# A fourth size class for experts of 65 to 96 tokens in a mixture-of-experts layer

## The reference

```python
logits = h @ w_router + b_router                 # h (320, 1024), 32 experts
top_val, top_idx = lax.top_k(logits, 4)
gates = softmax(top_val)
for each expert e, on the tokens that chose it:
    gu = xb @ w_gu[e] + b_gu[e]                  # 1024 -> 2048
    x_glu, x_lin = jnp.split(gu, 2, axis=-1)     # each clipped to 7
    act = x_glu * sigmoid(1.702 * x_glu) * (x_lin + 1.0)
    out = (act @ w_down[e] + b_down[e]) * gate   # 1024 -> 1024
    acc = acc.at[tok].add(out)
x = x + ga2 * acc
```

## Time and profile before

| what | value |
|---|---|
| time, median of 3 runs | 1476.66 us |
| profiled execution: its span, first to last instruction | 1473.6 us |
| TensorE matmuls busy | 1254.8 us, 85% |
| VectorE, ScalarE busy | 375.8 us, 217.6 us |
| bytes moved by DMA | 454.63 MB, mean 309 GB/s |
| instruction-fetch packets on queue q8 | 34, of 0.56 MB |
| chain that ended last | PE 68%, DMA 10%, SPq 7%, DVE 7%, issue 5% |

### The profile page before, as it was taken

One profiled execution on the slowest core, in us unless ns is written; L12 is line 12 of the kernel. 1 busy time (PEld: TensorE's weight loads), 2 busy tenths in 40 slices (PEclk: granted clock), 3 DMA queues, 4 the chain that ended last, 5 costly groups with the idle time before them and its releaser, 6 DMA issues.

```text
span 1473.6 us, 26636 instructions
## 1 busy us (share of the span) xinstructions
PE 1254.8 (85%) x10191; PEld 679.3 (46%) x10192; DVE 375.8 (26%) x1023; ACT 217.6 (15%) x482; POOL 29.3 (2%) x51
## 2 busy tenths in 40 slices
PE   3999999878677888788879998889999989978894
PEld 2677766653343334344434445344444443444442
DVE  1114435342111322111322123112222212321123
ACT  1323242131010101101101011010111111100100
POOL 0001110010000000000000000000000000000000
PEclk8999998887878989799989999999999999989996
DMA  9941327262999999996999969969999999999691
GB/s 361 353 150 58 102 85 286 76 236 92 377 372 387 387 387 387 387 387 234 384 387 387 348 234 386 386 236 385 387 377 378 364 387 387 387 387 387 229 382 55
DMA packets 230508, 454.63 MB, mean 309 GB/s; under 512 B 6941, under 2 KB 11677, under 8 KB 230429
## 3 DMA queue, kind: packets, MB, share of 16 engines
q1 hardware_dynamic: 222608, 448.02, 83.1%
q10 hardware_dynamic: 7852, 5.94, 1.3%
HBM read 450.77 MB, written 3.17 MB: 308 GB/s over the span
## 4 chain that ended last, share of the span: by engine, by line
PE 68%; DMA 10%; SPq 7%; DVE 7%; issue 5%; ACT 1%; DVEq 0%; ACTq 0%
PE psum L828 29%; PE psum L848 15%; PE psum L543 8%; DMA ring<-w_gu 8%; SPq L469 7%; PE psum L731 2%; PE psum L868 2%; DVE work L1492 2%; DMA ring<-w_ada 2%; PE psum L834 1%; PE psum L512 1%; PE psum L853 1%; PE psum L799 1%; PE psum L791 1%; DVE work L1476 1%
## 5 line engine op out<-in xcount | busy, mean ns | idle before, releaser
L828 PE MATMUL psum<-ring,work 128*32 128x256 f32 (+2 forms) x3008 | 440.4, 497 | 79.6 <-DMA ring<-w_gu 50.3
L828 PEld LDWEIGHTS psum<-ring,work 128*32 128x32 f32 (+2 forms) x3008 | 186.7, 135 | 309.1 <-issue 266.0
L848 PE MATMUL psum<-ring,work 128*32 128x128 f32 (+2 forms) x2880 | 234.8, 344 | 11.3 <-issue 9.6
L848 PEld LDWEIGHTS psum<-ring,work 128*32 128x32 f32 (+2 forms) x2880 | 145.8, 131 | 93.3 <-issue 66.1
L933 ACT ACTIVATE work<-psum 128x320 f32<-128x320 f32 (+4 forms) x238 | 93.0, 407 | 412.8 <-PE psum L848 248.8
L1476 DVE TENSOR_SCALAR work<-psum 128x128 f32<-128x128 f32 (+2 forms) x64 | 25.3, 395 | 504.2 <-PE psum L828 504.2
L543 PE MATMUL psum<-h,ring 128*128 128x320 f32 x448 | 126.5, 440 | 1.2 <-ACT h L977 1.2
L1147 ACT ACTIVATE work<-work 128x128 f32<-128x128 f32 (+2 forms) x64 | 25.1, 393 | 597.5 <-DVE work L1476 597.5
L1492 DVE TENSOR_TENSOR work<-psum,work 128x320 f32<-128x320 f32 x256 | 107.4, 477 | 16.5 <-PE psum L868 15.6
L543 PEld LDWEIGHTS psum<-h,ring 128*128 128x128 f32 x448 | 85.9, 193 | 36.9 <-issue 1.6
L1466 DVE TENSOR_SCALAR work<-csb 32x128 f32<-32x128 f32 x32 | 8.8, 274 | 343.8 <-PE psum L848 343.0
(11 more groups left out here) (231 smaller groups left out, 711.3 us busy)
## 6 DMA issues: line engine op xcount, KB each, us to landing
ring<-w_gu SPq DMA_DIRECT2D x128, 2048.0 KB, 15.4
ring<-w_down SPq DMA_DIRECT2D x64, 2048.0 KB, 16.7
ring<-w_ada SPq DMA_DIRECT2D x12, 2048.0 KB, 9.6
ring<-w_in SPq DMA_DIRECT2D x7, 2048.0 KB, 21.1
ring<-w_out SPq DMA_DIRECT2D x2, 2048.0 KB, 8.5
x<-xT ACTq DMA_DIRECT2D x1, 1280.0 KB, 13.3
yT<-h SPq DMA_DIRECT2D x4, 320.0 KB, 2.2
csb<-const ACTq DMA_DIRECT2D x1, 784.0 KB, 8.5
```

What stands on the lines that cost most here:

```text
L828: last = mm(o.rearrange("p (s n) -> p s n", s=2), l, r, start=kk == 0, stop=kk == KD)
L848: last = mm(bank[DN + i][m * g:m * (g + 1), 0:n], l, r, start=kk == 0, stop=kk == 8)
```

## The change

A fourth class, 3, is put between classes 1 and 2 for 65 to 96 tokens; class 1 is left for 97 to 128. In class 3 the first 64 tokens go through the layout of class 2 and the last 32 through that of class 4, one after the other on the same weights. The second part's `gate_up` writes bank 1 and waits for the bank's earlier reader. The selection matrix of the last 32 gets a buffer of its own (`wpick2`, `spread2`), scatter adds both parts in PSUM, and the gated unit works on 384 columns. Gather and the transposes of the tokens are class 1's. `turn_pick` comes behind a branch of its own. The gather of a class 1 or 3 expert waits for VectorE's last read of the banks. `by_size` asks up to three questions in place of two. On TensorE, VectorE and ScalarE alike the stream now holds four bodies at each branch.

```diff
         def by_size(eng, n, b, body):
 
 
-            with eng.If(n > b * CAP + CAP // 2):
+            with eng.If(n > b * CAP + 3 * CAP // 4):
                 body(1)
             with eng.Else():
-                with eng.If(n > b * CAP + CAP // 4):
-                    body(2)
+                with eng.If(n > b * CAP + CAP // 2):
+                    body(3)
                 with eng.Else():
-                    body(4)
+                    with eng.If(n > b * CAP + CAP // 4):
+                        body(2)
+                    with eng.Else():
+                        body(4)
...
@@ -781,6 +786,10 @@
             def gather(turn, groups):
 
 
+                if groups == 3:
+                    groups = 1
+                if groups == 1 and not (isinstance(turn, int) and turn == 0):
+                    pe.wait_ge(lc_ready, turn * 2)
                 m = CAP // groups
...
-                m = CAP // groups
-                parts = max(groups, 2)
-                n = CHC // parts
...
-                for kk in range(KD + 1):
-                    if kk == KD - 1 and i == 0:
-                        pe.wait_ge(eh_ready, turn + 1)
-                    for g in range(parts):
-                        o = psum[:, U + g, :] if groups == 1 else psum[m * g:m * (g + 1), U + i, 0:2 * n]
-                        if kk < KD:
-                            l, r = xg[:, kk, 0:m], both[:, :, kk, g * n:(g + 1) * n]
-                        else:
-                            b0 = i * CHC + g * n
-                            l, r = eh[0:NE, 0:m], biases[:, :, b0:b0 + n]
-                        last = mm(o.rearrange("p (s n) -> p s n", s=2), l, r, start=kk == 0, stop=kk == KD)
+                for t0, gr in (((0, 2), (64, 4)) if groups == 3 else ((0, groups),)):
+                    m = CAP // gr
+                    parts = max(gr, 2)
+                    n = CHC // parts
+                    if t0 and not (isinstance(turn, int) and turn == 0):
+                        pe.wait_ge(spread_ready, turn)
+                    if t0 and i:
+                        pe.wait_ge(lc_ready, turn * 2 + 1)
+                    for kk in range(KD + 1):
+                        if kk == KD - 1 and i == 0 and t0 == 0:
+                            pe.wait_ge(eh_ready, turn + 1)
+                        for g in range(parts):
+                            if t0:
+                                o = psum[m * g:m * (g + 1), X + 1, 2 * n * i:2 * n * (i + 1)]
+                            elif gr == 1:
+                                o = psum[:, U + g, :]
+                            else:
+                                o = psum[m * g:m * (g + 1), U + i, 0:2 * n]
+                            if kk < KD:
+                                l, r = xg[:, kk, t0:t0 + m], both[:, :, kk, g * n:(g + 1) * n]
+                            else:
+                                b0 = i * CHC + g * n
+                                l, r = eh[0:NE, 0:m], biases[:, :, b0:b0 + n]
+                            last = mm(o.rearrange("p (s n) -> p s n", s=2), l, r, start=kk == 0, stop=kk == KD)
                 last.then_inc(gu_ps, 1)
...
             def turn_act(i, turn, groups):
                 pe.wait_ge(act_ready, turn * 2 + (i + 1))
-                for c in range(4 // groups):
+                for c in range(3 if groups == 3 else 4 // groups):
                     last = nc.tensor.transpose(bank[R + i][:, c * P:(c + 1) * P], act[:, i, c * P:(c + 1) * P], ident)
                 last.then_inc(atr_ps, 1)
             def down(i, turn, groups):
-                m, n = CAP // groups, CHC // groups
...
-                for kk in range(9):
-                    for g in range(groups):
...
+                for t0, gr in (((0, 2), (64, 4)) if groups == 3 else ((0, groups),)):
+                    m, n = CAP // gr, CHC // gr
+                    o0 = 256 if t0 else 0
+                    for kk in range(9):
+                        for g in range(gr):
...
+                            last = mm(bank[DN + i][m * g:m * (g + 1), o0:o0 + n], l, r, start=kk == 0, stop=kk == 8)
                 last.then_inc(dn_ps, 1)
 
-            def turn_pick(turn):
-                for tt, (t0, n) in enumerate(TILES):
-                    last = nc.tensor.transpose(bank[X + 1][0:CAP, t0:t0 + n], wpick[0:n, tt, :], ident[0:n, 0:n])
+            def turn_pick(turn, groups):
+                for bk, src in (((X + 1, wpick), (X, wpick2)) if groups == 3 else ((X + 1, wpick),)):
+                    for tt, (t0, n) in enumerate(TILES):
+                        last = nc.tensor.transpose(bank[bk][0:CAP, t0:t0 + n], src[0:n, tt, :], ident[0:n, 0:n])
                 last.then_inc(str_ps, 1)
...
             def scatter(i, turn, groups):
 
 
-                m = CAP // groups
...
+                    for o0, gr in (((0, 2), (256, 4)) if groups == 3 else ((0, groups),)):
...
+                            c0_ = o0 + f * P - g * (CHC // gr)
+                            rows_ = slice(m * g, m * (g + 1))
+                            last = mm(bank[R + 2 * c + hf][:, 0:T], otok[rows_, i, c0_:c0_ + P], (spread2 if o0 else spread)[rows_, :],
+                                      start=o0 == 0, stop=o0 > 0 or groups != 3)
+                            if o0 or groups != 3:
+                                last.then_inc(sc_ps, 1)
...
                 by_size(pe, n, b, lambda groups: (down(0, turn, groups), down(1, turn, groups)))
                 pe.wait_ge(wpick_ready, turn * 3 + 3)
-                turn_pick(turn)
+                by_size(pe, n, b, lambda groups: turn_pick(turn, groups))
...
+            def spreads(turn, groups):
+                act_.wait_ge(str_ps, turn + 1)
+                if groups == 3:
+                    copy(spread2, bank[0][:, 0:T])
+                copy(spread, bank[1][:, 0:T]).then_inc(spread_ready, 1)
...
-                by_size(act_, n, b, lambda groups: outputs(turn, groups))
-                act_.wait_ge(str_ps, turn + 1)
-                copy(spread, bank[1][:, 0:T]).then_inc(spread_ready, 1)
+                by_size(act_, n, b, lambda groups: (outputs(turn, groups), spreads(turn, groups)))
...
 
-                n = CAP // groups
+                n = CAP // (1 if groups == 3 else groups)
...
+                    for r0, gr, dst in (((0, 2, wpick), (64, 4, wpick2)) if groups == 3 else ((0, groups, wpick),)):
+                        n = CAP // gr
+                        last = ts(dst[0:nt, tt, :].rearrange("p (g n) -> p g n", g=gr),
+                                  iota_c[0:nt, r0:r0 + n].unsqueeze(1).broadcast_to([nt, gr, n]),
+                                  rank[0:nt, tt, bass.ds(e, 1)], gate[0:nt, tt, bass.ds(e, 1)],
+                                  ALU.is_equal, ALU.mult)
+                    last.then_inc(wpick_ready, 1)
...
+                n = 384 if groups == 3 else CHC // groups
                 lc_ = lc[:, i, :]
-                ts(two(lc_), l_, SWIGLU_LIMIT, -SWIGLU_LIMIT, ALU.min, ALU.max).then_inc(lc_ready, 1)
+                if groups == 3:
+                    b0 = 256 * i
+                    ts(gc[:, 256:384], bank[1][:, b0:b0 + 128], SWIGLU_LIMIT, None, ALU.min)
+                    ts(gc[:, 0:256], bank[2 + i][:, 0:256], SWIGLU_LIMIT, None, ALU.min).then_inc(gc_ready, 1)
+                    ts(lc_[:, 256:384], bank[1][:, b0 + 128:b0 + 256], SWIGLU_LIMIT, -SWIGLU_LIMIT, ALU.min, ALU.max)
+                    ts(lc_[:, 0:256], bank[2 + i][:, 256:512], SWIGLU_LIMIT, -SWIGLU_LIMIT, ALU.min, ALU.max).then_inc(lc_ready, 1)
```

More of the change, by code:

```diff
@@ L190, in build @@
         spread = take4(T)
+        spread2 = take4(T)
         lgT = spread
@@ L199, in build @@
         act = res[:, 0:2, :]
+        wpick2 = res[:, 2, 0:3 * CAP].rearrange("p (t n) -> p t n", t=3)
         member = take4(3, NE)
@@ L797, in turn_x @@
                 pe.wait_ge(xtok_ready, turn + 1)
-                for c in range(8 // groups):
+                for c in range(8 // (1 if groups == 3 else groups)):
                     last = nc.tensor.transpose(psum[:, U + c // 4, c % 4 * P:(c % 4 + 1) * P], xtok[:, c * P:(c + 1) * P], ident)
@@ L862, in scatter @@
                         pe.wait_ge(acc_ready, turn * 8 + (2 * c + 3))
-                    for hf in range(2):
-                        f = 2 * hf + c
-                        g = f * groups // 4
-                        c0_ = f * P - g * (CHC // groups)
-                        rows_ = slice(m * g, m * (g + 1))
-                        mm(bank[R + 2 * c + hf][:, 0:T], otok[rows_, i, c0_:c0_ + P], spread[rows_, :],
-                           start=True, stop=True).then_inc(sc_ps, 1)
+                    for o0, gr in (((0, 2), (256, 4)) if groups == 3 else ((0, groups),)):
+                        m = CAP // gr
+                        for hf in range(2):
+                            f = 2 * hf + c
+                            g = f * gr // 4
+                            c0_ = o0 + f * P - g * (CHC // gr)
[4 more added lines that the diff above has]
```

(23 more changed lines are left out.)

33 lines of the change are left out of this document (14 added, 19 removed).

## The result

The changed kernel takes 2125.7 us (median of 4 runs, 2120.5 to 2132.2) where the kernel before takes 1477.4 beside it. The ratio is 1.4381, 95% interval 1.4346 to 1.4417: 44% slower. The forecast was 2200, by instructions that are fetched again in each execution of TensorE's loop.

The account below looks back on a forecast made before the run. Weights bound the loop within 6%, TensorE deciding in class 1 and 2 turns. Refetching adds 694 us in 30 turns, 20 in turn 0, 10 in turn 31: 1473.6 + 724 = 2198, given as 2200 us; range 1750 to 2550.

Parts of the forecast that it names:

- The mechanism: TensorE's loop body outgrows the held instruction blocks, the oldest goes first, so all are refetched every execution; chance 0.60.
- The trace shows eight blocks held: Reading of the fetch queue before: body over seven blocks of 256 instructions plus the one ahead, eight held at once.
- Twelve packets a turn at 57.7 us: Refetch in the loop's 30 turns: 12 instruction packets each, 1731 us for 1036.9, +694.
- The outer turns: Longer streams in turns 0 and 31, outside the loop: four more blocks fetched in turn 0, +20 us; turn 31 +10.
- The class 3 gain: In four turns of 65 to 96 tokens, shorter gate_up and down: net 10 us a turn, 40 us in four.
- The scatter in two layouts: In class 3 turns, twice the scatter matmuls, half in each layout: 0 to 1 us a turn, taken as 0.
- With all held: Rival: more than eight blocks fit or the fetch hides, so -40 + 11 = -29 us, 1448; chance 0.13.
- The questions: One more question at each branch, 0.12 us each: 0.8 us in some 14 turns that TensorE decides, +11 us.
- TensorE's matmul time: Sign: total matmul time on TensorE would fall by some 45 us despite the refetching.
- What would show it: Signs: some 390 packets on q8, some 220 GB/s, no weight waits, issue at turn heads and ahead of L869.

Follow-up runs that it names:

- e1: Changed kernel with class 3's question set so that no expert meets it and class 1 taking all above 64 tokens: 2133.8 us, ratio 1.4413.
- e4: Changed kernel without class 1, the four large experts in class 3, two questions in by_size: 2122.7 us, ratio 1.4338.
- e8: e6 with 82 never-executed transposes for 68 at the end of TensorE's loop body: 1976.5 us, ratio 1.3377.
- e9: e8 with 116 more never-executed transposes ahead of the loop: 1479.8 us, ratio 1.0016.
- e6: e5 with a second 68 never-executed transposes, ahead of the second gate_up: 1480.6 us, ratio 1.0029.
- e5: Kernel before with 68 never-executed transposes (136 instructions) at the end of TensorE's loop body: 1481.1 us, ratio 1.0033.
- w2: w1 with turn_pick and ScalarE's copy of the spread matrix put ahead of down: 1453.9 us, ratio 0.9835.
- w1: Kernel before with class 3 run through class 2's and class 4's shared code, and class 1 left out: 1459.6 us, ratio 0.9893.
- e7: Kernel before with one more question, guarding nothing, ahead of every by_size on TensorE, VectorE and ScalarE: 1491.7 us, ratio 1.0103.

## Why the prediction was right, point by point

**The mechanism** was the forecast's, and is shown: e1 rules out what is executed, e4 the number of questions, e8 against e9 leaves only the blocks. That the oldest block goes when another comes fits: a body one block over finds none of its blocks (nine packets in each of the turns 1 to 29 of e8, for eight blocks and the one behind). Whether "oldest" is the first fetched or the last used these loops cannot tell. The Trainium skill, "Advanced Engine Details and Errata" (ISA Cache), gives TensorE 128 KB in lines of 16 KB. The eight held blocks of e6 and e9 and the fall with a ninth agree with that; the same section's "Only 2 cache lines!" does not fit TensorE here. The Trainium skill, "Runtime: NRT & Kernel Launch" (instruction fetch mechanics), warns of the stall for a taken branch whose target is outside "the current 2-page window". The stall is seen here, the window is not: the loop of e6 jumps back over seven blocks without a fetch. The same section calls the cost of crossing a 16 KiB boundary "mostly hidden", of a stream that is fetched while it runs on. In the changed kernel, whose stream jumps, it was not: 687.7 us of "issue" stood ahead of five of TensorE's lines.

**"The trace shows eight blocks held"** was wrong by one. With the corrected count it was seven, so the kernel before had a whole block to spare. That eight is the limit all the same, as e6, e8 and e9 show, the trace of before did not tell: as a reading of that trace the number was luck. The forecast did not hang on it, because the body after, with the one ahead, is over the limit by three (by the forecast's count four). For a change of 200 instructions the same argument would have called a refetch where e5 and e6 show none.

**Twelve packets a turn at 57.7 us** were 11 at 55.7. A packet cost 57.7 / 12 = 4.81 us in the forecast and 55.7 / 11 = 5.06 in the run: two small errors that partly cancelled, so the time is nearer than the model deserves. The loop gave +634.4 for +694. e8 shows that a price per packet is the wrong form: at 5.06 its turn would be 45.5 us, and it was 51.2.

**The outer turns:** turn 0 +12.0 for +20, turn 31 and what follows +6.0 for +10. q8 has three packets more in turn 0 (9 for 6) and three more behind turn 30 (11 for 8), where the forecast took four. A block more in turn 0 thus cost 4.0 us, for 6.2 taken, and one in turn 31 some 2.

**The class 3 gain.** A `gate_up` over both parts was forecast at 12.25 us and took 12.25 and 12.24 in the turn of w2 that is shown. In the other three the second one took 12.27 and the first, behind a wait for the weights, 13.66 to 15.16. Both `down` together were forecast at 12.7 for 16.86 and took 14.77 in the turn shown, half the gain, and 13.55 to 14.78 in the other three. Most of what is missing is the clock, in the column after POOL:

```profile
852.57:856.21 3.64, 3.64 (x69) 3.03 (x72) 0.00 (x0) 0.77 (x2) 0.00 (x0) 0.50 1.05 387
856.72:858.70 1.98, 1.98 (x72) 1.78 (x72) 0.00 (x0) 0.00 (x0) 0.00 (x0) 0.97 0.00 0
```

These are the first 64 `down` records of that turn and the same 64 of the second half. In all, the four turns of w2 are 35.9 us shorter than before, for 40 forecast, and the turns behind them 7.3 longer. The scatter in two layouts, taken as 0, cost the 1.2 us a turn seen in w1. In the changed kernel little of the gain is left: e1, with the same class bodies in the stream, takes 70.7 to 72.9 us in the four turns for 67.1 to 68.3, and the ratios of the two kernels, 1.4413 and 1.4381, overlap in their intervals. With all held the prediction had 1448 (-29); w2 with two questions for three reached 1453.9 (-24).

**The questions:** +11 forecast, as 0.8 us in each of some 14 turns that TensorE decides, and +14.5 in e7, where the 15 turns of classes 1 and 2 in the loop are 1.0 us longer each and those of class 4 hide it. Form and size were right.

**TensorE's matmul time** was forecast to fall by 45 us and rose by 91.9 (1254.8 to 1346.7). This step was wrong. The forecast took the matmuls' durations from before, at the granted clock of 0.93 in the loop, and did not ask what gaps do to it: the loop after has 0.75. The same shapes after, from 350 us (busy, mean ns, idle before):

```profile
L847 PE MATMUL psum<-ring,work 128*64 128x512 f32 x1088 | 282.4, 678 | 172.5 <-issue 172.5
L847 PE MATMUL psum<-ring,work 128*32 128x256 f32 x2432 | 186.7, 474 | 198.6 <-issue 198.6
...
L869 PE MATMUL psum<-ring,work 128*32 128x128 f32 x2432 | 113.5, 352 | 117.2 <-issue 117.2
```

A class 4 `down` matmul takes 352 ns on average for 293 before. The stretches of e8 show how: behind 15.02 us of idle TensorE works at a granted clock of 0.55, then at 1.00. How much of the 91.9 us lay on the path is open, since fetches run beside the matmuls.

**What would show it** came as said in the rest: 365 packets for 390, 229 GB/s for 220, no wait for the experts' weights among the long waits, "issue" at each head and ahead of L869.

## What to carry to other kernels

Count the instructions of a loop's body on each engine, the jumped-over branches with the executed ones, and lay them over the blocks that the fetch queue's packets show; a body that touches so many blocks that they and the one fetched ahead are more than is held (eight here) pays in every execution. In the profile the sign is an instruction queue with packets in the steady part of the loop, "issue" ahead of the lines behind a jump, and falling GB/s with no wait for data. Here a new size class paid only once it shared the code of the classes that it is made of; leaving out class 1 alone (e4) did not do.

## What the runs showed of the hardware

- The fall is a step, not a slope: 1747 instructions in the body 1480.6 us, 1775 of them 1976.5 or 1479.8 us, by where the body begins. Branches that are never taken count in full.
- Where it falls, most of the added time stands at the head of the loop: "issue" ahead of `gate_up` is 441.8 us in e8 for 24.5 before, in 33 gaps of up to 16.0 us, and the loop is 500 us longer.
- TensorE comes back from idle at a lower granted clock: a stretch with 19.8 us of matmul work (turn 7 before, clock 0.92) has 25.5 us of it when it is broken by 11 us gaps (clock 0.66).
- Open: why single turns of the changed kernel bring 10 or 12 packets for 11, and which blocks the three or four packets in the 15 us at the loop's head of e8 bring. e5 and e6 are 3 to 4 us above before with intervals just off 1; whether the taken jump over dead code or the longer first pass makes it was not tried.
